# The Fourier stage of a two-block network on one Trainium2 core: casts and copies in another order, and the last gate tile in front of the output tiles

## What is computed

```python
def token_mix(h, w_in, w_fourier, w_ret, w_out):
    proj = h @ w_in
    u_f, q, k, v, g, a_f, a_r = jnp.split(proj, offsets, axis=-1)
    y_f = fourier_mix(u_f) @ w_fourier          # fft2 over tokens and groups of 128 features, real part
    y_r = retention_branch(q, k, v, g) @ w_ret
    merged = jax.nn.sigmoid(a_f) * y_f + jax.nn.sigmoid(a_r) * y_r
    return merged @ w_out
```

## Time and profile before

| | |
|---|---|
| median of three runs | 2933.72 us |
| the profiled execution's own time | 2932.58 us |
| its span in the profile | 2930.6 us |
| mean granted TensorE clock | 0.996 |
| TensorE (PE) busy | 2901.3 us, 99% of the span |
| Fourier stage of the first layer (from g3 to the end of o7) | about 1254.9 to 1358.7 us |
| of the second layer | about 2098.7 to 2201.3 us |

### The profile page before, as it was taken

How to read it: one execution, slowest core, us unless ns; L and a number is a source line. 1 busy time by engine, 2 the same in 40 slices (tenths; PEclk the granted TensorE clock), 3 DMA queues, 4 the chain that set the end, 5 groups by cost and what they waited for, 6 DMA issues and landing times.

```text
span 2930.6 us, 49393 instructions
## 1 busy us (share of the span) xinstructions
PE 2901.3 (99%) x19658; PEld 2428.4 (83%) x19658; DVE 1574.0 (54%) x2227; ACT 1103.3 (38%) x1671; POOL 1577.3 (54%) x1912
## 2 busy tenths in 40 slices
PE   9999999999999999999999999999999999999998
PEld 7877777788888888888888898888888888888887
DVE  5467777424555666775334265435753532473635
ACT  4454435233443332443433343323433342342323
POOL 6432233355546676656444556565475444575654
PEclk9999999999999999999999999999999999999999
DMA  5211111233326687433222223232333222233232
GB/s 172 93 45 41 42 55 56 95 137 101 126 90 225 236 281 252 154 115 122 83 90 76 95 87 109 92 102 87 98 123 122 71 85 87 94 94 100 94 101 72
DMA packets 92292, 322.21 MB, mean 110 GB/s; under 512 B 10144, under 2 KB 14368, under 8 KB 91808
## 3 DMA queue, kind: packets, MB, share of 16 engines
q1 hardware_dynamic: 84544, 302.39, 31.2%
q10 hardware_dynamic: 7520, 16.67, 1.7%
HBM read 315.09 MB, written 3.93 MB: 109 GB/s over the span
## 4 chain that ended last, share of the span: by engine, by line
PE 95%; issue 2%; POOL 1%; DVE 1%; DMA 0%; ACT 0%; POOLq 0%; SPq 0%; ACTq 0%; DVEq 0%
PE bank L900 25%; PE bank L904 24%; PE bank L901 24%; PE bank L1248 2%; PE bank L893 2%; PE bank L895 2%; PE bank L894 2%; PE bank L1259 2%; PE bank L1267 1%; POOL w_lo L831 1%; PE bank L928 1%; PE bank L929 1%; PE bank L930 1%; PE bank L1775 1%; PE bank L1774 1%
## 5 line engine op out<-in xcount | busy, mean ns | idle before, releaser
L831 POOL TENSOR_TENSOR w_lo<-w_raw,w_hi 128x256 fp32r<-128x256 f32 x1768 | 1448.5, 852 | 993.4 <-ACT w_hi L1852 987.3
L900 PE MATMUL bank<-act,w_hi 128*128 128x512 f32 (+1 forms) x3464 | 1314.8, 380 | 4.7 <-POOL w_lo L831 2.6
L904 PE MATMUL bank<-act,w_lo 128*128 128x512 f32 (+1 forms) x3464 | 1293.7, 373 | 0.0
L901 PE MATMUL bank<-act,w_hi 128*128 128x512 f32 (+1 forms) x3464 | 1292.6, 373 | 0.1
L900 PEld LDWEIGHTS bank<-act,w_hi 128*128 128x128 f32 x3464 | 653.2, 189 | 126.2 <-issue 8.8
L904 PEld LDWEIGHTS bank<-act,w_lo 128*128 128x128 f32 x3464 | 652.8, 188 | 115.3 <-issue 0.3
L901 PEld LDWEIGHTS bank<-act,w_hi 128*128 128x128 f32 x3464 | 653.7, 189 | 107.1 <-issue 0.5
L1852 ACT CAST w_hi<-w_raw 128x1024 fp32r<-128x1024 f32 (+1 forms) x446 | 462.7, 1043 | 336.7 <-DMA w_raw<-in_weights 153.3
L1860 ACT ACTIVATE arena<-bank 128x512 f32<-128x512 f32 (+1 forms) x177 | 104.3, 592 | 418.2 <-PE bank L904 401.6
L849 POOL TENSOR_TENSOR stats<-stats,exponent 128x8 f32<-128x8 f32 (+2 forms) x38 | 46.5, 1225 | 302.6 <-DVE stats L2895 150.0
L2581 DVE TENSOR_TENSOR act<-tmp,act 128x512 fp32r<-128x512 f32 (+1 forms) x140 | 122.1, 872 | 77.4 <-ACT act L1879 72.7
(11 more groups left out here) (357 smaller groups left out, 3092.0 us busy)
## 6 DMA issues: line engine op xcount, KB each, us to landing
w_raw<-in_weights SPq DMA_DIRECT2D x471, 512.0 KB, 3.5
arena<-in_ada SPq DMA_DIRECT2D x96, 512.0 KB, 4.8
arena<-in_strips ACTq DMA_DIRECT2D x8, 448.0 KB, 3.6
arena<-in_x ACTq DMA_DIRECT2D x1, 2048.0 KB, 10.5
y_scratch<-tmp ACTq DMA_DIRECT2D x7, 256.0 KB, 2.0
arena<-y_scratch ACTq DMA_DIRECT2D x1, 1792.0 KB, 8.1
arena<-in_dft ACTq DMA_DIRECT2D x2, 777.5 KB, 4.1
arena<-in_x SPq DMA_DIRECT2D x3, 512.0 KB, 7.5
```

What stands on the lines that cost most here:

```text
L831: ins = nc.gpsimd.tensor_tensor(w_lo[:, k, cols], weights_of(u)[:, cols], w_hi[:, k, cols].bitcast(F32), ALU.subtract)
L900: nc.tensor.matmul(o, wh, xh, start=first, stop=False)
L901: nc.tensor.matmul(o, wh, xl, start=False, stop=False)
L904: mm = nc.tensor.matmul(o, wl, xh, start=False, stop=last)
```

## The change

It makes nine edits, all in the Fourier stage, in both layers. g7 moves in front of o0, in PE's order and in the order of the units, and ACT takes its gate before o0's copy. ACT loads the sigmoid table with a 1 x 1 activation before the first fold's cast. It casts g5 after the second fold's cast, E0 before the seventh's, and O0 before the eighth's. `take_folded` copies its tile first and then casts ahead. Behind `high_spectrum(2)` the casts go up to o2, and o3's comes after g6's gate. For j below 4 the loop over output tiles no longer calls `follow`. On DVE output_sums(4) moves before low_spectrum(3), and output_sums(5) behind `f_rows`. The third product of the features takes the last token spread to 128 equal columns as its weights, where it had one column.

```diff
-FOURIER_ORDER += [("gate", 6), "out"] + [("out", j) for j in range(4)] + [("gate", 7)] + [("out", j) for j in range(4, 8)]
+FOURIER_ORDER += [("gate", 6), "out", ("gate", 7)] + [("out", j) for j in range(8)]
...
-                    for o, rows in ((banks[4][:, 0:WAVES], slice(0, P)), (banks[4][:, WAVES:2 * WAVES], slice(P, 2 * P)),
-                                    (banks[4][0:1, 2 * WAVES:3 * WAVES], slice(2 * P, 2 * P + 1))):
-                        nc.tensor.matmul(o, x[:, rows], COS_FEATURE, start=True, stop=True)
+                    last = x[:, 2 * P:2 * P + 1].to_broadcast([P, P])
+                    for b, tokens in enumerate((x[:, 0:P], x[:, P:2 * P], last)):
+                        nc.tensor.matmul(banks[4][:, WAVES * b:WAVES * (b + 1)], tokens, COS_FEATURE, start=True, stop=True)
...
                 def take_folded(what):
                     t = plan.folded[l][what]
-                    follow(t)
                     tile_done(act, t)
...
                     ins.then_inc(sem(f"bank_free{bank_of(t)}"), 1)
+                    follow(t)
...
+                nc.scalar.activation(X_MIDDLE[0:1, HALF_WAVES:EVEN], prm("g_final")[0:1, :], ACT.Sigmoid)
                 folded_high(0)
                 folded_high(1)
+                cast_to(OPENING_GATES[l])
...
                 take_gate(3)
+                cast_to(SUM_UNITS[(KT + KT // 2) * l])
                 folded_high(6)
-                cast_to(SUM_UNITS[(KT + KT // 2) * l])
+                cast_to(SUM_UNITS[(KT + KT // 2) * l] + 1)
                 folded_high(7)
...
-                cast_to(SUM_UNITS[(KT + KT // 2) * l + KT // 2 + 3])
+                cast_to(SUM_UNITS[(KT + KT // 2) * l + KT // 2 + 2])
                 take_features(3)
                 take_gate(6)
-                cast_to(GATE_UNITS[l])
+                cast_to(SUM_UNITS[(KT + KT // 2) * l + KT // 2 + 3])
                 high_spectrum(3)
...
+                take_gate(7)
                 for j in range(KT):
-                    follow(FOURIER_TILES[KT * l + j])
+                    if j >= 4:
+                        follow(FOURIER_TILES[KT * l + j])
...
-                    if j == 3:
-                        take_gate(7)
...
+                output_sums(4)
                 low_spectrum(3)
-                output_sums(4)
-                output_sums(5)
...
                                     NYQUIST[0:KT, 0:HALF_WAVES].bitcast(F32), ALU.subtract), "f_rows")
+                output_sums(5)
```

More of the change, by code:

```diff
@@ L579, in build_program @@
         BY_VECTOR = [VALUE_UNITS[3], VALUE_UNITS[6], tiles[stages["x_q"][0] + 1]["blocks"][0][0]]
-        GATE_UNITS = [tiles[plan.gates[f"fourier_out{l}"][0][KT - 1]]["blocks"][0][0] for l in range(LAYERS)]
+        OPENING_GATES = [tiles[plan.gates[f"fourier_out{l}"][0][5]]["blocks"][0][0] for l in range(LAYERS)]
         MIDDLE_UNITS = [tiles[plan.folded[l]["middle"]]["blocks"][0][0] for l in range(LAYERS)]
```

## The result

Over 20 runs of each the changed kernel took 2939.22 us (2937.54 to 2940.92) and the kernel before 2934.33 us: a ratio of 1.0016, 95% interval 1.0009 to 1.0023. It is 4.9 us slower, on the side I forecast, about half of the 9.2 us of my sum, and by my own limit of 0.2% (5.9 us) still within "no change". The profiled execution has a span of 2936.0 us where before had 2930.6, so 5.4 us are to be found in the traces. The mean granted clock is 0.997.

The account below looks back on a forecast made before the run. TensorE, busy 99% of the span, bounds the kernel, so only its stops and low-clock stretches count. Terms -6.2 up to tokens(2), +6.0 and +1.6 to tokens(3), +7.8 output tiles sum to +9.2 us: 2942, range 2929 to 2949.

Parts of the forecast that it names:

- E0: Tile in the Fourier stage's opening: its low part on POOL ends at 1272.4, not 1277.05; PE wants it at 1274.2.
- The third product: Features' weights going from one column to 128: up to 2 us won or 1.7 lost; taken as nothing.
- The openings: Start of the Fourier stage: both early stops go; tokens(0) at 1289.2, first layer gains 7.7 us.
- Tokens(2): Features(2) on DVE ends at 1312.1, PE stops 4.2 us; gain left 3.5 us first layer, 2.7 second.
- the same chain ends at the same place relative to m: Second layer before tokens(2): chain of loads and sums timed as in the first layer; gain left 2.7 us.
- Tokens(3): Output_sums(3) waits for o1's low part: tokens(3) 12.0 us after tokens(2), 3.0 us lost in each layer.
- for the clock: At tokens(3): the second stop may lower the clock again; half of 1.6 us a layer, +1.6 in all.
- The output tiles: Stops of 0.75 us before o5, 2.5 before o6, half-clock stretch of 1.6, less 0.95: 3.9 us lost a layer.
- the hidden `f_rows`: At o0's last matmul: g7 in front hides the wait for `f_rows`, saving 0.9 to 1.0 us a layer.
- The second one: Rival, no change: the new stops come but the clock mostly holds through them; +1.4 us, 2935; chance 0.28.
- The first, 2925: Rival, faster: o1 loaded early enough for features(2) to end when PE reaches tokens(2); 8.3 us faster, 2925; chance 0.12.
- E1: Tile before tokens(0): its low part, behind O0's on POOL, as tight as DVE's chain; 1.2 us for both.

Follow-up runs that it names:

- the best kernels with g7 in either place: g7 put back, features(2) before output_sums(1), two ACT/DVE waits removed: 2914.78 us; changed kernel, g7 in front, DVE's and ACT's orders fitted: 2917.00 us.

## Why the prediction was right, and where it was not

**The openings: right.** E0's low part ends at 1271.8 and PE comes to it at 1274.28, 2.5 us later, where I had 2. I put all that was lost before E0, 2.98 and 4.4 us, down to its low part; part of it was m waiting for DVE's last folds (0.61 us in the first layer, 1.47 and 0.62 in the second). These waits went too, since DVE no longer waits for O0 ahead of those folds (3.18 and 4.11 us before), so the sum was not hurt. The table load shows as 1.28 us beside idle time, with the next activation 1.29 us behind its start and no further drain. The Trainium skill ("ScalarE: Activation LUTs", What ACT_TABLE_LOAD costs) has 2.66 us with the drain; the trace decides against it here. Tokens(0) came at 1288.76 for my 1289.2.

**Tokens(2): right in kind, wrong in the second layer.** I had 1312.1 in the first layer, with a stop of 4.2 us; it came at 1312.61 after 4.79. That output_sums(1) is the last thing it waits for is shown by moving features(2). As I had it, DVE stands waiting before both sums, 4.80 us for o0 and 0.77 for o1 in the first layer. The step that failed is "the same chain ends at the same place relative to m". The gain left there was 4.8 us and not 2.7. What I had not counted: the residual steps of DVE (L3416) exist in the first layer only. input_sums(3) (L3378) starts 2.47 us after tokens(0) in the first layer, behind two of these steps, and 0.86 us after it in the second, so the chain to o1 starts 1.6 us sooner there. The next two low parts on POOL, those of O3 and g6, then take 5.56 us and not 6.47, with no residual steps beside them (first rows: first layer; then second):

```profile
1288.74 2.46 DVE L3416 SCALAR_TENSOR_TENSOR arena<-arena,params,square_sum 128x512 f32<-128x512 f32 x2
1291.23 1.64 DVE L3378 TENSOR_TENSOR arena<-w_raw 128x1024 f32<-128x1024 f32 x1
```

```profile
2134.98 0.15 DVE L3439 TENSOR_TENSOR arena<-bank,arena 1x2 f32<-1x2 f32 x1
2136.04 1.66 DVE L3378 TENSOR_TENSOR arena<-w_raw 128x1024 f32<-128x1024 f32 x1 [0.92 <-POOL w_lo L831]
```

Of the 3.8 us by which my sum was too high in the spans this term has 2.1, tokens(3) has 0.8 and the output tiles have 1.4. The first layer up to tokens(2) was 0.5 us worse than I had it.

**Tokens(3): right.** 12.53 and 12.29 us behind tokens(2), for my 12.0. The stops are 1.78 and 1.77 us, the rest is tokens(2) at half clock. The further 0.8 us a layer "for the clock" did not come: behind these stops it held.

**The output tiles: right, but for the clock.** The stops of 0.75 and 2.5 us measured 0.64 and 2.20 us, with 0.16 us beside each from start to start. The half clock behind o6 came in one layer of two. Of my 3.9 us a layer, 2.44 and 3.99 were paid; the kernel with g7 alone moved paid 3.9 and 4.0. Moving the two sums one join earlier took o6's stop away and left one before o5. I gave the hidden `f_rows` to g7 alone. g7 alone moved does hide it, but with g7 put back the other edits hide it too. Since the change does both, the sum was not touched.

**The third product: taken as nothing, rightly.** Its worth is 0.26 to 0.29 us a call, 2.2 us in all, just above my bound of 2. I had said that every call stands before a stop; in the changed kernel three of the four of a layer do so directly, and what features(1) wins runs into the stop before tokens(2). It can pay once the stops are gone.

**The rivals.** The second one, that the clock mostly holds, gave 2935 and the forecast 2942. What happened lies between them: the clock fell in three of the six places where I charged it. I had given 0.60 to a time above 2939.6, and 2939.22 lies just below that: the loss is real, but smaller than what I took to be likeliest. The first, 2925, would have needed o1 early. With g7 put back DVE gets o1 at 1306.58 and not at 1309.20, and 2.02 us of stop are left. That kernel does not pay the rival's 9.7 us in the output tiles either; without them the rival's sum gives 2916, and the kernel took 2919.25.

## What to carry to other kernels

In a chain of engines with few buffers, a tile that is moved forward also pushes every load behind it back by one place in the ring. The price is paid at the next step that waits for one of those loads, or stands behind such a step on an in-order engine, and in this kernel it was larger when the rest arrived sooner. Before undoing such a move, look at what stands in front of the late step on each in-order engine: here a few lines in another order took the price of the move from 20 us to 2.2, that between the best kernels with g7 in either place. And two gains in front of the same late step don't add up; the step that is next must be priced each time.

## What the runs showed of the hardware that I had not expected

- **The same stop lowers the clock or not.** o6's start waits 2.19 or 2.20 us in both layers of four kernels (the changed one, g7 alone moved, features(2) earlier, casts first for late pairs). Six of the eight were followed by a low clock. A stop of 2.85 us before tokens(2) was (0.59 above), one of 2.85 before tokens(3), in the kernel with features(2) earlier, was not. What decides is open. Half a stretch of low clock is a fair price for such a stop only as an average.
- **A matmul whose weights have one column delays its neighbours.** The five products of a features call take 0.26 to 0.29 us less when the third has 128 equal columns and not one, though it then multiplies 128 times as much. All eight calls together are too little to be told in 2934 us, but the trace has it in every call.
- **One load, two durations.** E2 and O2 reached DVE 5.0 us after POOL turned to E1's low part before, and 6.8 us after it with g7 alone moved, though nothing ahead of them differs. A forecast that rests on one such row can be 2 us out from this alone.
